# Loading and splitting the first pooled rows inside the scan phase of a hybrid mLSTM and pooling block

## The chip, the cores and the metric

The kernel runs on one core of one Trainium2 chip. The metric is the device time of one execution in microseconds, the median of several runs. All times inside an execution are microseconds from its first instruction.

## What is computed

One layer over 2048 latent tokens of 1024 channels, in float32. A modulated RMSNorm feeds one input projection. Its columns go to two branches: a bidirectional chunked mLSTM scan and a pooling mixer on a grid of 32 x 64 tokens. What matters here is the pooling branch and the merge that follows both:

```python
mixed = (jnp.stack(groups, axis=-2) - pg)                      # four box means of 128 channels each, less the input
mixed = jnp.einsum('btgc,gcd->btgd', mixed, pool_w)            # one 128 x 128 matrix for each group
y_p   = (mixed * pool_scale * silu(z_p)) @ branch_p_w          # 512 -> 1024
hn    = h * rsqrt(mean(h * h) + EPS)                           # by head, h is the scan's output
y_m   = (hn * head_norm_w * sigmoid(o) * silu(z_m)) @ branch_m_w
out   = rmsnorm(x + gate * ((sigmoid(g_m) * y_m + sigmoid(g_p) * y_p) @ out_w))
```

## The kernel before

**Number format.** Every matrix product is made of three passes over fp32r operands: an operand is split into a high part (a copy, mostly by ScalarE) and a low part (the value less its high part, by VectorE or GpSimd), and high by high, high by low and low by high are summed in PSUM. A "split" below is this pair of instructions. Line 42's `f32` only reads such a tile as float32.

**Phases.** The kernel is a row of blocks, and a block ends when all engines have reached its end. The change touches the last two.

**The scan phase** (lines 1545 to 2227) has 136 slots of some 7 us. Slots 8 to 135 each do one step of the mLSTM scan (one head, one direction, one chunk of 128 tokens) and a share of the projection pieces that were left over. In each slot SyncE (SP) issues, in this order, the values and queries of the step three slots on (`values`, `queries`), the scores of that step (`load_scores`), the stores of the pieces that ended in the slot before (`store_piece`), the store of the step before (`store_h`) and the load of the other direction's output for the next step (`other_direction`, L1744). ScalarE prepares the next step's operands, evacuates pieces, writes the high part of the step's weights (`weights_hi`) and then copies the step's result out of PSUM (`ysb`, L1995). VectorE makes the low parts, updates the state and finishes the step (`finish`, whose last instruction L2092 adds the other direction's output). GpSimd computes the four box means one after the other (L2192 to L2227), paced by the steps, and stores each to `mix_d`; the last store is issued in slot 128. After its last slot SP waits until all stores of the projection and of the scan have landed (L1798 to L1801), and only then is its part of the block done.

**The last phase** (lines 2231 to 2926) goes over the tokens in four quarters of 512. A quarter has eight pooled units (the product with `branch_p_w`, one for each 128 channels, 12 matmuls), eight hidden units (with `branch_m_w`, 24 matmuls) and eight output units. Each engine's instructions stand in an order written out by hand. For the first quarter it is this:

- SP loads the pooling weights (`pw`), the pooled rows and their gate rows group by group (`pooled`: `mixt` and `zpt`, two buffers each, L2357 and L2358), and between them the hidden rows (`hidden`, L2344), their gates (`hidden_gate`, `ut`, L2350), the sigmoid gates (`gate_p`, L2370), two tiles of weights (`tile(2)`, `tile(3)`, L2335) and a row of the final norm. The pooled rows of groups 2 and 3 wait until a buffer is free.
- ScalarE writes the high part of `pw`, copies the residual gate's row out of PSUM, then alternates the high parts of the pooled rows (`pooled_hi`, L2614) and of the gated groups (`branch_hi`, L2620). Then come the squares of the first hidden rows (`squares`, L2590 to L2593), their scaling (`normalise`, L2600) and the high part of weight tile 2 (`split_hi`, L2582).
- GpSimd writes the low parts of the pooled rows and of the gated groups (L2899, L2903).
- TensorE turns the residual gate into a row (L2554), multiplies the four groups (`group`, L2467, three matmuls each into two banks in turn), then runs pooled units 0 and 1 (L2475), turns the first hidden rows (`turn_hidden`, L2454), runs units 2 and 3, and so on.
- VectorE writes the low part of `pw`, gates the four groups into one buffer `ypt` (`branch`, L2746; a group waits until the one before is split), and for each pair of units makes the low part of a weight tile (`split_lo`, L2719), applies the sigmoid gates (`gate_pooled`, L2756, which waits for `turn_hidden`) and gates the hidden rows (`gate_hidden`, L2736).

Unit 2 reuses the bank of unit 0, so it waits for `gate_pooled` of unit 0, which stands behind `split_lo` of weight tile 2 on VectorE.

Of the kernel before, what the change touches and what calls it, by code (L numbers as in the profile page):

```python
# [7 lines left out]
FP32 = mybir.dt.float32  # L8
# [3 lines left out]
P = 128  # L12
# [34 lines left out]
def hybrid_block(nc, x, c, ctx, c_ctx, norm_w, ada_w, ada_b, in_w, gate_b, head_norm_w, pool_w,  # L47
# [32 lines left out]
    with ExitStack() as top:  # L80
# [1464 lines left out]
        with ExitStack() as ph:  # L1545
# [8 lines left out]
            QS, KS, VS, SS = 4, 3, 4, 4  # L1554

# [29 lines left out]
            icnt = sb("icnt", [P, 2, GRID_W])  # L1585

# [89 lines left out]
            def _(sp):  # L1676
# [219 lines left out]
            def _(act):  # L1896
# [64 lines left out]
                for t in range(NSLOT):  # L1961
# [266 lines left out]

        late.close()

        with ExitStack() as ph:
# [6 lines left out]
            pw = sb("pw", [P, PG, P])  # L2238
            pw_h = sb("pw_h", [P, PG, P], FP32R)
            pw_l = sb("pw_l", [P, PG, P], FP32R)  # L2240
# [3 lines left out]
            yt = sb("yt", [P, KT, P])  # L2244
            y_h = sb("y_h", [P, KT, TQ], FP32R)
            y_l = sb("y_l", [P, KT, TQ], FP32R)
            mixt = sb("mixt", [P, 2, TQ])
# [8 lines left out]
            m_h = sb("m_h", [P, KT, TQ], FP32R)  # L2256
            m_l = sb("m_l", [P, KT, TQ], FP32R)
            og = sb("og", [P, 2, 2 * P])
# [4 lines left out]
            hss = sb("hss", [P, 4, 2, HEADS])  # L2263
# [5 lines left out]
            rows_loaded = [sem(f"rows_loaded{n}") for n in range(2)]; gate_turned = sem("gate_turned")  # L2269
            gate_ready = sem("gate_ready")   # L2270
            pw_hi = sem("pw_hi"); pw_lo = sem("pw_lo")
# [5 lines left out]
            mix_hi = sem("mix_hi"); mix_lo = sem("mix_lo"); mix_done = sem("mix_done")  # L2277
# [19 lines left out]
            ASIDE = bank[6]  # L2297

# [29 lines left out]
            def _(sp):  # L2328
# [24 lines left out]
                def pooled(i, g):  # L2353
                    n = i * PG + g
                    if n >= 2:
                        sp.wait_ge(yp_made, n - 1)
# [42 lines left out]
                tile(3)  # L2399
                hidden(0, 3)  # L2400
                hidden_gate(0, 1)
                sp.dma_start(fn_row[:, :], final_norm_w.partition_broadcast(P)).then_inc(rows_loaded[1], 16)
# [44 lines left out]
            def _(pe):  # L2447
# [10 lines left out]
                def group(i, g):  # L2458
# [3 lines left out]
                    if c >= 2:  # L2462
                        pe.wait_ge(yp_made, c - 1)
                    if i:
                        pe.wait_ge(p_gated, i * KT)
                    for n, (a, b) in enumerate(((pw_h, mix_h), (pw_h, mix_l), (pw_l, mix_h))):
                        mm = pe.matmul(bank[2 + g % 2][:, :], a[:, g, :], b[:, g % 2, :], start=(n == 0), stop=(n == 2))  # L2467
# [83 lines left out]


# [4 lines left out]
                pe.wait_ge(pw_lo, 1)  # L2557
                for g in range(PG):
                    group(0, g)
# [17 lines left out]
            def _(act):  # L2577
# [31 lines left out]
                def pooled_hi(i, g):  # L2609
                    c = i * PG + g  # L2610
                    act.wait_ge(mix_loaded[g % 2], 32 * (c // 2 + 1))
                    if c >= 2:
                        act.wait_ge(mix_done, c - 1)
                    act.activation(mix_h[:, g % 2], mixt[:, g % 2], ACT.Copy).then_inc(mix_hi, 1)  # L2614

                def branch_hi(i, g):
# [3 lines left out]
                    act.activation(yp_h[:, g], ypt[:, :], ACT.Copy).then_inc(yp_hi, 1)  # L2620
# [26 lines left out]
                act.wait_ge(rows_loaded[0], 16)  # L2647
                act.activation(pw_h[:, :, :], pw[:, :, :], ACT.Copy).then_inc(pw_hi, 1)
                act.wait_ge(gate_turned, 1)
                for b in range(2):  # L2650
                    row = act.activation(gate_row[:, b * TQ:(b + 1) * TQ], bank[6 + b][:, :], ACT.Copy)
                row.then_inc(gate_ready, 1)
                pooled_hi(0, 0)
                pooled_hi(0, 1)
                branch_hi(0, 0)
                pooled_hi(0, 2)
                branch_hi(0, 1)
                pooled_hi(0, 3)
                branch_hi(0, 2)
                squares(0, 0)  # L2660
                branch_hi(0, 3)
                normalise(0, 0)
                for i in range(NTQ):
                    for t in range(NT5):
# [3 lines left out]
                        if t < M0:  # L2668
                            if i == 0:
# [3 lines left out]
                                if t + 1 < QT:  # L2673
                                    normalise(0, t + 1)
                            else:
# [39 lines left out]
            def _(dve):  # L2715
# [24 lines left out]
                def branch(i, g):  # L2740
                    c = i * PG + g
                    dve.wait_ge(mix_done, c + 1)
                    if c:
                        dve.wait_ge(yp_hi, c)
                        dve.wait_ge(yp_lo, c)
                    dve.scalar_tensor_tensor(out=ypt[:, :], in0=bank[2 + g % 2][:, :],  # L2746
                                             scalar=vcol[:, VR["pool"] + g:VR["pool"] + g + 1], in1=zpt[:, g % 2],
                                             op0=ALU.mult, op1=ALU.mult).then_inc(yp_made, 1)
# [81 lines left out]
                dve.wait_ge(pw_hi, 1)  # L2830
                dve.tensor_tensor(pw_l[:, :, :], pw[:, :, :], f32(pw_h[:, :, :]), ALU.subtract).then_inc(pw_lo, 1)
                branch(0, 0)
                branch(0, 1)
                branch(0, 2)
                branch(0, 3)
                norms(0, 0)
                for i in range(NTQ):
                    for t in range(NT5):
# [20 lines left out]
                        elif t < T_O:  # L2859
                            n = t - M0  # L2860
                            if i == 0 and n == 0:
                                dve.wait_ge(rows_loaded[1], 16)
# [28 lines left out]
            def _(pool):  # L2891
# [13 lines left out]
                pooled_lo(0, 0)  # L2905
                pooled_lo(0, 1)
                branch_lo(0, 0)
                pooled_lo(0, 2)
                branch_lo(0, 1)
                pooled_lo(0, 3)  # L2910
                branch_lo(0, 2)
                branch_lo(0, 3)
# [39 lines left out]
```

## Time and profile before

| | us |
|---|---|
| median of 3 runs | 2403.62 (2403.3 to 2408.27) |
| profiled execution, its own time | 2401.29 |
| its span, first to last instruction | 2399.5 |
| TensorE busy in the span | 2274.2 (95%) |
| VectorE, ScalarE, GpSimd busy | 1494.0, 972.8, 610.1 |
| data moved by DMA | 501.66 MB, 209 GB/s on average |

The profiled execution is one run, and its span is 1.79 us shorter than its own time. The page cuts the span into 40 slices of 60 us. TensorE is busy for nine tenths or more in most of them; two of the few exceptions after the start, with busy shares of six and nine tenths and a clock of seven tenths in the first, hold the end of the scan phase and the start of the last phase, around 1860 us.

### The profile page before, as it was taken

The numbers are of one execution on the slowest core, as the hardware profiler recorded it, in microseconds if no ns is written. First come the engines' busy times: TensorE is split into PE (matmuls) and PEld (weight loads), VectorE is DVE, ScalarE is ACT, GpSimd is POOL, SyncE is SP. The second block draws the span as 40 slices with busy tenths as digits, with TensorE's granted clock in tenths as the row PEclk, the third lists the DMA queues.
The fourth block names the chain that finished last, engine by engine and source line by source line (L and its number), as shares of the span: only waits on it lengthen the run. The fifth ranks groups of instructions, "written<-read, shape, count | busy, mean of one in ns | idle before, by whom it ended". The sixth has DMA issues, their size and how long they took to land. (4 is left out here: it accounts for less than half of the span.)

```text
span 2399.5 us, 35270 instructions
## 1 busy us (share of the span) xinstructions
PE 2274.2 (95%) x12251; PEld 1934.1 (81%) x12251; DVE 1494.0 (62%) x2660; ACT 972.8 (41%) x1982; POOL 610.1 (25%) x545
## 2 busy tenths in 40 slices
PE   7799999989999989999999999999999699999998
PEld 5588888767887878888888888888887488888878
DVE  5545567875766646575767566767675355646564
ACT  6323355542332323434444344444443535252532
POOL 0223344533445421121122112321220212020210
PEclk9899999999999999999999999999999799999999
DMA  9466698876788666666776877666665665757562
GB/s 273 143 154 176 180 250 242 255 218 136 192 201 249 163 223 224 222 221 215 233 250 201 274 262 250 224 221 200 227 211 188 206 192 158 234 171 226 187 207 100
DMA packets 399266, 501.66 MB, mean 209 GB/s; under 512 B 25800, under 2 KB 283380, under 8 KB 393588
## 3 DMA queue, kind: packets, MB, share of 16 engines
q1 hardware_dynamic: 334836, 377.76, 48.0%
q10 hardware_dynamic: 55136, 83.90, 14.0%
q0 software_dynamic: 9120, 37.75, 6.0%
q8 instruction: 101, 1.65, 0.3%
q14 instruction: 73, 0.60, 0.1%
HBM read 352.82 MB, written 163.27 MB: 215 GB/s over the span
## 5 line engine op out<-in xcount | busy, mean ns | idle before, releaser
L1867 PE MATMUL bank<-xlate,wh 128*128 128x512 f32 x2048 | 670.4, 401 | 10.1 <-DVE v_t L2001 6.3
L1867 PEld LDWEIGHTS bank<-xlate,wh 128*128 128x128 f32 x2048 | 373.1, 189 | 79.4 <-DVE v_t L2001 6.7
L1867 PE MATMUL bank<-xlate,wl 128*128 128x512 f32 x1024 | 409.6, 400 | 0.0
L1016 PE MATMUL bank<-xlate,wh 128*128 128x512 f32 x1024 | 330.4, 396 | 5.8 <-DVE wl L1288 4.9
L1016 PE MATMUL bank<-xtop,wh 128*128 128x512 f32 x768 | 250.6, 403 | 9.9 <-DVE wl L1288 9.9
L1016 PEld LDWEIGHTS bank<-xlate,wh 128*128 128x128 f32 x1024 | 191.1, 189 | 48.1 <-ACT wh L1068 4.7
L1867 PEld LDWEIGHTS bank<-xlate,wl 128*128 128x128 f32 x1024 | 193.4, 189 | 34.1
L1016 PE MATMUL bank<-xlate,wl 128*128 128x512 f32 x512 | 201.4, 393 | 0.0
L1016 PEld LDWEIGHTS bank<-xtop,wh 128*128 128x128 f32 x768 | 144.2, 192 | 41.8 <-ACT wh L1068 10.8
L2024 DVE SCALAR_TENSOR_TENSOR state<-state,cols,bank 128x516 f32<-128x516 f32 x128 | 95.7, 748 | 112.0 <-PE bank L1828 111.9
L1016 PE MATMUL bank<-xtop,wl 128*128 128x512 f32 x384 | 152.7, 398 | 0.0
L1312 DVE SCALAR_TENSOR_TENSOR tmp<-bank,psum 128x512 f32<-128x512 f32 x112 | 76.9, 687 | 104.3 <-PE bank L1016 64.0
L1995 ACT ACTIVATE ysb<-bank 128x258 f32<-128x258 f32 x128 | 49.5, 387 | 197.4 <-PE bank L1828 196.9
L2029 DVE TENSOR_TENSOR wl<-wraw,wh 128x1024 fp32r<-128x1024 f32 x62 | 77.2, 1245 | 67.6 <-ACT wh L1915 67.6
L917 POOL TENSOR_TENSOR os<-tmp,os 128x512 fp32r<-128x512 f32 x64 | 90.1, 1412 | 111.6 <-ACT os L1177 111.5
L1068 ACT ACTIVATE wh<-ssum 128x512 fp32r<-128x512 f32 x96 | 60.4, 629 | 138.9 <-PE bank L1016 75.2
L1841 PE MATMUL bank<-state_h,q_t 128*128 128x258 f32 x512 | 113.0, 283 | 2.6 <-DVE den L2081 2.6
L1016 PEld LDWEIGHTS bank<-xlate,wl 128*128 128x128 f32 x512 | 96.6, 189 | 21.7
L1828 PE MATMUL bank<-v_t,ek_h 128*128 128x258 f32 x576 | 110.3, 283 | 1.7 <-DVE ek_l L2006 1.7
L1288 DVE TENSOR_TENSOR wl<-ssum,wh 128x512 fp32r<-128x512 f32 x96 | 78.7, 820 | 44.9 <-ACT wh L1068 44.7
L1932 ACT ACTIVATE s_t<-bank 128x128 f32<-128x128 f32 x64 | 17.7, 277 | 193.6 <-PE bank L1818 193.5
L1841 PEld LDWEIGHTS bank<-state_h,q_t 128*128 128x128 f32 x512 | 87.5, 189 | 8.9 <-issue 3.3
(321 smaller groups left out, 5351.4 us busy)
## 6 DMA issues: line engine op xcount, KB each, us to landing
v_t<-vk_d SPq DMA_DIRECT2D x144, 384.0 KB, 3.8
qk_d<-os SPq DMA_DIRECT2D x32, 1024.0 KB, 5.7
q_t<-qk_d SPq DMA_DIRECT2D x128, 256.0 KB, 4.1
wraw<-wpair_d ACTq DMA_DIRECT2D x31, 1024.0 KB, 6.6
rawb<-in_in_w_dram ACTq DMA_DIRECT2D x64, 256.0 KB, 5.4
vk_d<-os SPq DMA_DIRECT2D x16, 1024.0 KB, 4.6
wpair_d<-in_in_w_dram POOLq DMA_DIRECT2D x64, 256.0 KB, 6.1
k_t<-qk_d SPq DMA_DIRECT2D x64, 256.0 KB, 5.0
```

What stands on the lines that cost most here:

```text
L917: pool.tensor_tensor(part[:, :, 1, :], tmp[:, a % NTM].rearrange("p (c t) -> p c t", t=P), f32(part[:, :, 0, :]), ALU.subtract).then_inc(q ...
L1016: mm = pe.matmul(dst[:, :], a[:, kd, :], x_block(part, XB[name])[:, kd], start=(kd == 0 and n == 0), stop=(kd == KH - 1 and n == 2))
L1068: act.activation(op_ring(wh, p), op_source(u, name), ACT.Copy).then_inc(op_hi, 1)
L1288: dve.tensor_tensor(op_ring(wl, p), op_source(u, name), f32(op_ring(wh, p)), ALU.subtract).then_inc(op_lo, 1)
L1312: return dve.scalar_tensor_tensor(out=dst, in0=src[:, :], scalar=kscale(u), in1=in1, op0=ALU.mult, op1=ALU.add)
L1828: mm = pe.matmul(ubank[:, b, 0:VW], e_[:, L, b * P:(b + 1) * P], v_t[:, V, va, :], start=(n == 0), stop=(n == 2))
L1841: pe.matmul(XBANK[:, 0:VW], q_t[:, l % QS, b, qa, :], c_[:, L, b, :], start=(b == 0 and n == 0), stop=(b == HB - 1 and n == 2))
L1867: mm = pe.matmul(bank[m % 2][:, :], a[:, u % 2, k, :], xlate[part][:, BLOCK_OF[k // KH, tq], k % KH], start=(k == 0 and n == 0), stop=(k = ...
L1932: act.activation(s_t[:, l % SS, :], SBANK[l % 2][:, 0:P], ACT.Copy).then_inc(s_copied, 1)
L1995: act.activation(ysb[:, :], YBANK[:, 0:VW], ACT.Copy).then_inc(y_read, 1)
L2024: dve.scalar_tensor_tensor(out=state[:, ch], in0=state[:, ch], scalar=col(d, NC + latent_chunk(l), 4, h), in1=upair[:, :, 0:VW], op0=ALU.m ...
L2029: dve.tensor_tensor(wl[:, u % 2], wpair[:, :, u % 2 * P:(u % 2 + 1) * P], f32(wh[:, u % 2]), ALU.subtract).then_inc(w_lo, 1)
```

## The change

Loads, splits and order of the first quarter's pooled part change; all quarters after it stay as they were.

- In slots 128, 129 and 130 SP also issues the loads of `pw` (256 KB), of the first quarter's pooled rows of all four groups (`mixq`, 1 MB) and of their gate rows (`zpq`, 1 MB), into scan buffers that are no longer used. The second waits for the last store of GpSimd to `mix_d`, the third for the last use of the buffer that it overwrites.
- ScalarE writes the high part of `pw` in slot 130 and of the four groups in slots 131 to 134, between `weights_hi` and the copy to `ysb`. GpSimd, whose box means are done, writes the five low parts.
- At the scan's end SP waits only for one of the two sets of step stores. The last step's store is waited for in the last phase, behind the load of the first `hidden_gate` and ahead of the first `hidden`.
- In the last phase TensorE does the four groups first, into four banks (2, 3, 0, 1), without waits between them, and then the residual gate's rows. VectorE gates a group in place (`zpq`) and writes its low part itself (`first_branch_lo`); ScalarE writes only the high parts of the gated groups, and copies the residual gate's row after the fourth hidden rows. GpSimd has nothing to do until the hidden rows.
- SP's order becomes: `hidden_gate(0,0)`, the wait, `hidden(0,0)`, `hidden(0,1)`, `gate_p(0,0)`, `gate_p(0,1)`, `hidden_gate(0,1)`, `tile(2)`, `hidden(0,2)`, `tile(3)`, `hidden(0,3)`, the final norm's row.

```diff
+            HEAD_AT, HEAD_SPLIT = NSLOT - 8, NSLOT - 5
@@ sync, scan phase
+                    if t == HEAD_AT:
+                        sp.wait_ge(s_done, NHALF)
+                        sp.dma_start(pw[:, :, :], pool_w[0].rearrange("g c n -> c g n")).then_inc(pw_loaded, 16)
+                    if t == HEAD_AT + 1:
+                        sp.wait_ge(mix_stored, 16 * PG)
+                        sp.dma_start(mixq[:, :, :], mix_d[:, :, 0:TQ].rearrange("g p t -> p g t")).then_inc(mixq_loaded, 16)
+                    if t == HEAD_AT + 2:
+                        sp.wait_ge(u_made, nz[-1])
+                        sp.dma_start(zpq[:, :, :], zp_d[:, :, 0:TQ].rearrange("g p t -> p g t")).then_inc(zpq_loaded, 16)
...
-                    sp.wait_ge(h_stored[n], 16 * NL // 2)
+                sp.wait_ge(h_stored[NL % 2], 16 * NL // 2)
@@ scalar, scan phase, after weights_hi
+                    if t == HEAD_SPLIT - 1:
+                        act.wait_ge(pw_loaded, 16)
+                        act.activation(pw_h[:, :, :], pw[:, :, :], ACT.Copy).then_inc(pw_hi, 1)
+                    if 0 <= t - HEAD_SPLIT < PG:
+                        g = t - HEAD_SPLIT
+                        act.wait_ge(mixq_loaded, 16)
+                        act.activation(mixq_h[:, g], mixq[:, g], ACT.Copy).then_inc(mix_hi, 1)
@@ gpsimd, scan phase, at the end
+                pool.wait_ge(pw_hi, 1)
+                pool.tensor_tensor(pw_l[:, :, :], pw[:, :, :], f32(pw_h[:, :, :]), ALU.subtract).then_inc(pw_lo, 1)
+                for g in range(PG):
+                    pool.wait_ge(mix_hi, g + 1)
+                    pool.tensor_tensor(mixq_l[:, g], mixq[:, g], f32(mixq_h[:, g]), ALU.subtract).then_inc(mix_lo, 1)
@@ sync, last phase
-                sp.dma_start(pw[:, :, :], pool_w[0].rearrange("g c n -> c g n")).then_inc(rows_loaded[0], 16)
-                pooled(0, 0)
-                pooled(0, 1)
+                hidden_gate(0, 0)
+                sp.wait_ge(h_stored[(NL - 1) % 2], 16 * NL // 2)
                 hidden(0, 0)
                 hidden(0, 1)
-                hidden_gate(0, 0)
                 gate_p(0, 0)
                 gate_p(0, 1)
-                pooled(0, 2)
+                hidden_gate(0, 1)
+                tile(2)
                 hidden(0, 2)
-                pooled(0, 3)
-                tile(2)
                 tile(3)
                 hidden(0, 3)
-                hidden_gate(0, 1)
@@ tensor, last phase
+            def group_bank(i, g):
+                return bank[2 + g % 2] if i else bank[(2, 3, 0, 1)[g]]
...
+                pe.wait_ge(pw_lo, 1)
+                for g in range(PG):
+                    group(0, g)
                 for j in range(KT):
                     mm = pe.matmul(bank[6 + j // 4][:, j % 4 * P:(j % 4 + 1) * P], mgate[:, j:j + 1].broadcast_to([P, P]),
                                    ident[:, :], start=True, stop=True)
                 mm.then_inc(gate_turned, 1)
-                pe.wait_ge(pw_lo, 1)
-                for g in range(PG):
-                    group(0, g)
@@ scalar, last phase
-                pooled_hi(0, 0) ... branch_hi(0, 3), with squares(0, 0) ahead of the last
+                for g in range(PG):
+                    branch_hi(0, g)
                 squares(0, 0)
+                act.wait_ge(yp_lo, PG)
                 normalise(0, 0)
@@ vector, last phase
+                def first_branch_lo(g):
+                    dve.wait_ge(yp_hi, g + 1)
+                    dve.wait_ge(yp_made, g + 1)
+                    dve.tensor_tensor(yp_l[:, g], zpq[:, g], f32(yp_h[:, g]), ALU.subtract).then_inc(yp_lo, 1)
...
                 branch(0, 0)
                 branch(0, 1)
-                branch(0, 2)
-                branch(0, 3)
+                for g in range(PG):
+                    first_branch_lo(g)
+                    if g + 2 < PG:
+                        branch(0, g + 2)
                 norms(0, 0)
```

## Rows read from the trace of the kernel before

**Rows 1.** Windows: us, busy us (count) of each engine, clock, DMA share, GB/s.
```profile
1859.70:1883.60 23.90, 8.61 (x25) 5.98 (x25) 2.94 (x4) 6.73 (x14) 7.58 (x7) 0.57 0.93 288
1859.70:1893.90 34.20, 17.89 (x60) 13.12 (x60) 5.96 (x10) 14.31 (x34) 10.05 (x8) 0.64 0.76 237
```

**Rows 2.** Chain of waits that ended last, around 1860: start us, us, what.
```profile
1860.72 5.45 DMA zpt<-zp_d
...
1873.99 7.58 DMA zpt<-zp_d
```

**Rows 3.** Timeline of SP's queue: start us, us, engine line op.
```profile
1857.57 0.32 SPq L1738 DMA_DIRECT2D hsum_d<-num  x1
1859.73 0.39 SPq L2387 DMA_DIRECT2D pw<-in_pool_w_dram  x1
```

**Rows 4.** DMA issues, 1855 to 1887 and 1798 to 1830: KB each, us to landing.
```profile
hsum_d<-num SPq DMA_DIRECT2D x1, 128.0 KB, 1.7
...
mix_d<-pool_a POOLq DMA_DIRECT2D x1, 1024.0 KB, 9.9
```

**Rows 5.** Timeline of TensorE, start of the last phase.
```profile
1859.77 3.75 PE L2554 MATMUL bank<-ident,mgate 128*128 128x128 f32 x16 [5.47 <-PEq L1545]
1868.31 0.77 PE L2467 MATMUL bank<-mix_h,pw_h 128*128 128x512 f32 x1 [4.79 <-POOL mix_l L2899]
...
1891.94 1.03 PE L2454 MATMUL bank<-ident,hsum 128*128 128x128 f32 x8
1893.95 0.47 PE L2475 MATMUL bank<-yp_h,wh 128*128 128x512 f32 x1 [0.98 <-DVE hsum L2756]
```

**Rows 6.** Timeline of ScalarE, start of the last phase.
```profile
1870.75 0.63 ACT L2620 ACTIVATE yp_h<-ypt 128x512 fp32r<-128x512 f32 x1 [1.69 <-DVE ypt L2746]
...
1882.64 0.40 ACT L2590 ACTIVATE junk_h<-hsum 128x256 bf16<-128x256 f32 x1
...
1886.81 1.69 ACT L2600 ACTIVATE hsum<-hsum,hss 128x256 f32<-128x256 f32 x4
1888.41 1.04 ACT L2582 ACTIVATE wh_c<-wraw 128x1024 fp32r<-128x1024 f32 x1
```

**Rows 7.** Timeline of VectorE, start of the last phase.
```profile
1869.96 0.75 DVE L2746 SCALAR_TENSOR_TENSOR ypt<-bank,vcol,zpt 128x512 f32<-128x512 f32 x1 [6.29 <-PE bank L2467]
...
1889.48 1.23 DVE L2719 TENSOR_TENSOR wl_c<-wraw,wh_c 128x1024 fp32r<-128x1024 f32 x1 [2.89 <-ACT wh_c L2582]
1893.11 1.28 DVE L2756 SCALAR_TENSOR_TENSOR hsum<-gt,bank 128x512 f32<-128x512 f32 x2 [2.40 <-PE bank L2454]
1900.65 1.28 DVE L2756 SCALAR_TENSOR_TENSOR hsum<-gt,bank 128x512 f32<-128x512 f32 x2
```

**Rows 8.** Windows of the scan's last slots, columns as in rows 1.
```profile
1800.00:1815.00 15.00, 15.00 (x81) 12.89 (x80) 8.29 (x23) 4.81 (x12) 0.43 (x1) 1.00 0.96 326
1815.00:1830.00 15.00, 15.00 (x81) 12.91 (x80) 10.30 (x24) 6.68 (x14) 0.00 (x0) 1.00 0.57 190
```

**Rows 9.** Timelines of GpSimd, SP, VectorE and ScalarE in the scan's last slots.
```profile
1799.83 0.59 POOL L2226 DMA_DIRECT2D mix_d<-pool_a  x1 [0.30 <-POOL pool_a L2224]
...
1814.91 0.43 SPq L1744 DMA_DIRECT2D hother<-h_d  x1
...
1827.99 0.49 DVE L2092 SCALAR_TENSOR_TENSOR num<-num,den,hother 128x256 f32<-128x256 f32 x1
...
1826.17 0.39 ACT L1995 ACTIVATE ysb<-bank 128x258 f32<-128x258 f32 x1 [1.23 <-PE bank L1828]
```

**Rows 10.** Windows where TensorE's granted clock changes, columns as in rows 1.
```profile
1854.30:1856.70 2.40, 0.00 (x0) 0.00 (x0) 2.33 (x5) 0.39 (x1) 0.00 (x0) 1.00 0.15 57
1856.70:1863.40 6.70, 3.63 (x16) 3.48 (x16) 1.19 (x4) 0.63 (x1) 0.00 (x0) 0.50 0.39 113
```

**Rows 11.** Timelines of GpSimd and VectorE: two splits at the same time.
```profile
1919.44 2.34 POOL L2894 TENSOR_TENSOR y_l<-yt,y_h 128x1024 fp32r<-128x1024 f32 x1 [4.97 <-ACT y_h L2607]
...
1920.34 2.52 DVE L2719 TENSOR_TENSOR wl_c<-wraw,wh_c 128x1024 fp32r<-128x1024 f32 x1 [2.07 <-ACT wh_c L2582]
```

More of the change, by code:

```diff
@@ L1585, in hybrid_block @@
             icnt = sb("icnt", [P, 2, GRID_W])
+            zpq = nc.alloc_sbuf_tensor_at("zpq", [P, PG, TQ], FP32, offset=TANH_AT)
+            pw = nc.alloc_sbuf_tensor_at("pw", [P, PG, P], FP32, offset=KEYS_AT)
+            pw_h = nc.alloc_sbuf_tensor_at("pw_h", [P, PG, P], FP32R, offset=KEYS_AT + PG * P * 4)
+            pw_l = nc.alloc_sbuf_tensor_at("pw_l", [P, PG, P], FP32R, offset=KEYS_AT + 2 * PG * P * 4)
+            mixq = nc.alloc_sbuf_tensor_at("mixq", [P, PG, TQ], FP32, offset=POOL_AT)
+            mixq_h = nc.alloc_sbuf_tensor_at("mixq_h", [P, PG, TQ], FP32R, offset=POOL_AT + PG * TQ * 4)
+            mixq_l = nc.alloc_sbuf_tensor_at("mixq_l", [P, PG, TQ], FP32R, offset=POOL_AT + 2 * PG * TQ * 4)
+            pw_loaded = sem("pw_loaded"); zpq_loaded = sem("zpq_loaded"); mixq_loaded = sem("mixq_loaded")
+            pw_hi = sem("pw_hi"); pw_lo = sem("pw_lo"); mix_hi = sem("mix_hi"); mix_lo = sem("mix_lo")
             piece_done = sem("piece4_done")
@@ L2244, in hybrid_block @@
             yt = sb("yt", [P, KT, P])
+            og = sb("og", [P, 2, 2 * P])
+            hss = sb("hss", [P, 4, 2, HEADS])
+            pad5 = sb("pad5", [P, 16])
+            pw_place = sb("pw_place", [P, 3, PG, P])
             y_h = sb("y_h", [P, KT, TQ], FP32R)
             y_l = sb("y_l", [P, KT, TQ], FP32R)
+            m_h = sb("m_h", [P, KT, TQ], FP32R)
+            m_l = sb("m_l", [P, KT, TQ], FP32R)
             mixt = sb("mixt", [P, 2, TQ])
@@ L2268, in hybrid_block @@
             unit_done = sem("unit_done")
-            rows_loaded = [sem(f"rows_loaded{n}") for n in range(2)]; gate_turned = sem("gate_turned")
+            rows_loaded = sem("rows_loaded"); gate_turned = sem("gate_turned")
             gate_ready = sem("gate_ready")
-            pw_hi = sem("pw_hi"); pw_lo = sem("pw_lo")
             h_loaded = [sem(f"h_loaded{n}") for n in range(QT)]
@@ L2354, in pooled @@
                     n = i * PG + g
[L2355 removed]
+                    if n >= PG + 2:
                         sp.wait_ge(yp_made, n - 1)
@@ L2461, in group @@
                     pe.wait_ge(mix_lo, c + 1)
-                    if c >= 2:
+                    if i:
                         pe.wait_ge(yp_made, c - 1)
-                    if i:
                         pe.wait_ge(p_gated, i * KT)
-                    for n, (a, b) in enumerate(((pw_h, mix_h), (pw_h, mix_l), (pw_l, mix_h))):
-                        mm = pe.matmul(bank[2 + g % 2][:, :], a[:, g, :], b[:, g % 2, :], start=(n == 0), stop=(n == 2))
+                    h, l, at = (mix_h, mix_l, g % 2) if i else (mixq_h, mixq_l, g)
+                    for n, (a, b) in enumerate(((pw_h, h), (pw_h, l), (pw_l, h))):
+                        mm = pe.matmul(group_bank(i, g)[:, :], a[:, g, :], b[:, at, :], start=(n == 0), stop=(n == 2))
                     mm.then_inc(mix_done, 1)
@@ L2645, in tail_root @@
                     act.activation(oss[:, 2, q:q + 1], oss[:, 1, q:q + 1], ACT.Sqrt).then_inc(tail_act, 1)
[L2647 to L2659, printed above, removed]
+                for g in range(PG):
+                    branch_hi(0, g)
                 squares(0, 0)
-                branch_hi(0, 3)
+                act.wait_ge(yp_lo, PG)
                 normalise(0, 0)
@@ L2674, in _ @@
                                     normalise(0, t + 1)
+                                if t == M0 - 1:
+                                    act.wait_ge(gate_turned, 1)
+                                    for b in range(2):
+                                        row = act.activation(gate_row[:, b * TQ:(b + 1) * TQ], bank[6 + b][:, :], ACT.Copy)
+                                    row.then_inc(gate_ready, 1)
                             else:
@@ L2742, in branch @@
                     dve.wait_ge(mix_done, c + 1)
-                    if c:
+                    scale = vcol[:, VR["pool"] + g:VR["pool"] + g + 1]
+                    if i:
                         dve.wait_ge(yp_hi, c)
                         dve.wait_ge(yp_lo, c)
-                    dve.scalar_tensor_tensor(out=ypt[:, :], in0=bank[2 + g % 2][:, :],
-                                             scalar=vcol[:, VR["pool"] + g:VR["pool"] + g + 1], in1=zpt[:, g % 2],
-                                             op0=ALU.mult, op1=ALU.mult).then_inc(yp_made, 1)
+                        dve.scalar_tensor_tensor(out=ypt[:, :], in0=group_bank(i, g)[:, :], scalar=scale, in1=zpt[:, g % 2],
+                                                 op0=ALU.mult, op1=ALU.mult).then_inc(yp_made, 1)
+                    else:
+                        if g == 0:
+                            dve.wait_ge(zpq_loaded, 16)
+                        dve.scalar_tensor_tensor(out=zpq[:, g], in0=group_bank(i, g)[:, :], scalar=scale, in1=zpq[:, g],
+                                                 op0=ALU.mult, op1=ALU.mult).then_inc(yp_made, 1)
+                def first_branch_lo(g):
+                    dve.wait_ge(yp_hi, g + 1)
+                    dve.wait_ge(yp_made, g + 1)
+                    dve.tensor_tensor(yp_l[:, g], zpq[:, g], f32(yp_h[:, g]), ALU.subtract).then_inc(yp_lo, 1)
                 def gate_pooled(i, n):
```

30 lines of the change are left out of this document (7 added, 23 removed).

## The prediction

> **What bounds the kernel now.** TensorE is busy for 95% of the span, so a gain can only come from a stretch in which it waits. I read the page's 40 slices first: the weak one is where the scan ends. Then the windows of that stretch: from the last phase's first instruction at 1859.70 to 1883.60 the DMA engines are 0.93 busy while TensorE has 8.61 us of work in 23.90, at a mean clock of 0.57 [rows 1]. Then the chain of waits: between 1860 and 1886 its longest members are two landings of `zpt`, 5.45 and 7.58 us, the gate rows of groups 0 and 3 [rows 2]; the splits of the four groups hang between them. So the stretch is bound by loads and by small steps that depend on them. From pooled unit 2 on (1893.95 [rows 5]) each pair of units is paced by TensorE and by a ring through ScalarE and VectorE that the change leaves alone. The working therefore asks one question: when does pooled unit 2 start after the change?
>
> **Step 1, the scan's end.** Before, the last step's store goes out at 1857.57 [rows 3] and lands 1.7 us later [rows 4], at 1859.27; SP's first issue of the new phase follows at 1859.73 [rows 3], 0.46 later. After, SP waits for the landing of older stores only: its queue is free at 1857.57 + 0.32 = 1857.89, and the phase starts at 1858.35, 1.38 us earlier. The bounds of this step are 0, if another engine holds the block, and 1.38; I take 1.38, since VectorE's last scan instruction is what SP's last store waits for. TensorE starts 0.04 behind SP, as before: 1858.39.
>
> **Step 2, the groups.** Nothing that they need is still to come, and each has a bank of its own. TensorE's clock has fallen by then: after 2.4 us of idling it went to 1.2 GHz, and came back 3.6 us after work began again (1859.77 to 1863.4 [rows 5, 10]). 512 columns at 1.2 GHz are 0.427 us, a group of three 1.28. From a group's start to VectorE's gating is 1.65 us (1868.31 to 1869.96 [rows 5, 7]): group 0 is gated at 1860.04, group 3, three times 1.28 later, at 1863.88. The low parts that VectorE now makes lie between: four gatings of 0.75 and four low parts of about half of 1.23 [rows 7] are 5.5 us, and the last ends near 1866. From gating to high part is 0.79 us (1869.96 to 1870.75 [rows 6, 7]), so ScalarE's last high part, 0.63 long [rows 6], runs from 1864.67 to 1865.3. TensorE meanwhile: the 12 group matmuls to about 1862.9 (the clock is back at 1862.0), the 16 of the residual gate (3.75 us at the low clock [rows 5], so 1.9) to 1864.8, and 24 matmuls of units 0 and 1 at 512 columns / 2.4 GHz, 5.1 us, to 1869.9, with no wait inside, as the fourth split is read some 2 us into unit 0.
>
> **Step 3, from the squares to unit 2.** Before, ScalarE began the squares at 1882.64, the scaling at 1886.81 (4.17 later) and weight tile 2 at 1888.41 (1.60 later) [rows 6]; VectorE's low part began 1.07 later, at 1889.48, for 1.23 [rows 7]. After, `gate_pooled` comes directly behind it, and unit 2 starts 0.84 after that (1893.11 to 1893.95 [rows 5, 7]). Sum: 4.17 + 1.60 + 1.07 + 1.23 + 0.84 = 8.91. From 1865.3 that is 1874.2. TensorE's turn (1.03 us [rows 5]) can only begin when the scaling ends, 1871.1; it ends at 1872.1, and TensorE idles 2.1 us, less than the 2.4 after which the clock fell. The copies of the residual gate's row, moved behind the fourth hidden rows, cost nothing: ScalarE waits there, and their first reader is the first merge. Without that cover it would be twice 0.63 at most.
>
> **Step 4, the loads.** The first 3.15 MB in SP's new order (`ut`, two `hsum`, two `gt`, `ut`, weight tile 2) must land before 1871.1. A store of 0.13 MB took 1.7 us [rows 4], of which 0.45 are bytes at 288 GB/s, so I let 1.2 us pass before the first bytes: 1859.55. At 288 GB/s, the rate of the saturated stretch [rows 1], 3.15 MB take 10.9 us: 1870.5, early by 0.6. At 237, the mean of the longer stretch [rows 1], 13.3: 1872.85, late by 1.8. I take the first, since the queue stays full; more speed gains nothing, as ScalarE comes later. The first `hsum` (1.05 MB with `ut`) is there at 1863.2, ahead of the squares. The sigmoid gate of unit 2, 6.03 MB in all with the final norm's row and weight tile 4, lands at 1880.5, against a use 6.70 us after unit 2's start (1893.95 to 1900.65 [rows 5, 7]), 1880.9. These two margins, 0.6 and 0.4, are the thin part of the forecast.
>
> **Step 5, what the scan pays.** ScalarE gets five high parts of 0.63, GpSimd five low parts of about half of 2.34 [rows 11], SP three issues. ScalarE idles 1.23 us ahead of `ysb` in a slot that also splits a weight tile [rows 9], which hides one high part; without that, 5 x 0.63 = 3.2. SP's wait in slot 129: the store to `mix_d` goes out at 1799.83 [rows 9] and lands 9.9 us later [rows 4], near 1810. Queued behind the wait are the issues of slot 130; the last of them, the other direction's rows, went out at 1814.91 and is used by the instruction at 1827.99 [rows 9], 13.1 us later. The 2.36 MB of loads are 8.2 us at 288 GB/s. The DMA engines are 0.96 busy from 1800 to 1815 and 0.57 from there to 1830 [rows 8]: 0.6 us are free in the first stretch, 6.4 in the second, so transfers of these slots may land some 4 us later; with the 7.58 of a queued load [rows 2] that is 11.6, within 13.1. Bounds: 0 and 8.2. I take 0, as TensorE is busy without a gap through the saturated 15 us [rows 8].
>
> **The sum.** Unit 2 starts at 1874.2 in place of 1893.95: 19.7 us, 1.4 from step 1 and 18.3 from steps 2 to 4. The profiled execution's own time, 2401.29, would be 2381.6. The median of the runs is 2403.62, 2.3 above that execution, so I predict 2383.9.
>
> **A rule against it.** VectorE's split of a weight tile took 2.52 us while GpSimd's split of hidden rows ran beside it [rows 11], and 1.23 alone [rows 7]. The Trainium skill, in "GPSIMD Engine Reference", section "1. Specifications", has the reason: GpSimd shares its SBUF interfaces with VectorE, and they contend when a VectorE instruction has two SBUF inputs. By that rule, the trace agrees. Five GpSimd splits in the scan could then hold VectorE; what that gives is rival 3.
>
> **The rivals.** (1) *The loads set the start.* At 237 GB/s unit 2's gate lands at 1859.55 + 25.4 = 1885.0, 4.1 late; TensorE idles over 2.4 us, its clock falls, and half of 3.6 us, 1.8, is lost. Gain 13.8: 2389.8. For it: SP's list leaves no slack, and the final norm's row lies ahead of that gate. Against it: 2.36 MB that were loaded here are gone. (2) *The waits only move.* If `mixq` lands after slot 131's high part is due, near 1825, ScalarE stands ahead of `ysb` and the scan is late one for one; the gain is gone if it lands at 1845. With 9.9 for the store and 7.58 for a queued load [rows 2, 4] it lands at 1817. Time: 2403.6. (3) *GpSimd holds VectorE in the scan.* Five times 1.29 (2.52 less 1.23), all on the path: gain 13.3, 2390.3. Against it: VectorE has 8.29 us of work in 15 [rows 8], and GpSimd starts when ScalarE's high part ends, in the slot's idle time. (4) *Slower: the early loads starve the scan.* If in each of slots 129 to 135 the other direction's rows land later than their lead of 13.1 us by 2.4 or more, TensorE idles, its clock falls and 1.8 is lost at half speed: 7 x 4.2 = 29.4 lost against 19.7 won, 2413.3. It decides from a landing of 15.5 us. Against it: 7.58 was the longest landing of the chain in a full queue [rows 2]. The Trainium skill, in "DMA: Bandwidth & Descriptors", section "Queues, rings and completion order", speaks for it: a completion is counted only after all earlier writes of the same DMA engine, so a small load waits for the whole megabyte ahead of it. No run here shows that by itself.
>
> **How the numbers follow.** Forecast, a gain of 16 to 23: 0.76, by itself 2380 to 2388. Rival 1: 0.12. Rival 2: 0.03. Rival 3: 0.04. Rival 4: 0.03. The last 0.02 is a small gain of any other cause. Within 0.2% (4.8 us, about what a measurement of this kernel can tell from no change) are rival 2 and half of the last: 0.04. Slower is rival 4: 0.03. Faster is the rest: 0.93. The range: at best TensorE alone sets the pace, and unit 2 starts at 1869.9 + 1.03 + 0.98 [rows 5] = 1871.9, a gain of 22 and 2379.3 from the profiled execution; at the other end stand rivals 1 and 3, 2390.3. So 2379 to 2391.
>
> **What would show it.** Right: SP's first issue of the last phase 0.8 us after the last step's store goes out; 12 group matmuls in a row; no landing of pooled rows in the chain before the second quarter; unit 2 some 16 us after the phase's first instruction, where it was 34 before; the scan's slots as long as before. Wrong, step by step: a longer gap at the block's end (step 1), waits of TensorE between the groups (2), weight tile 2 or the gates landing after ScalarE and VectorE ask for them (4), TensorE idling in slots 129 to 135 (5).

## The result and the profile after

Six runs of each kernel: 2390.87 us after (2386.77 to 2395.74) against 2405.69 before, a ratio of 0.9942, 95% interval 0.9929 to 0.9956. The forecast was 2383.9, with 2379 to 2391. The direction and the place were right, the size was not: 14.8 us instead of 19.7, and below the 16 to 23 to which the prediction gave 0.76. The profiled execution of the changed kernel took 2392.69 us, span 2390.9.

In this execution the scan ran 2.72 us later than in the profile of before, already ahead of its first changed load (the store to `mix_d` went out at 1802.56, where it was 1799.83 [rows 9]), so 2.72 is taken off when times of the two are compared. The head of the last phase first. SP's queue, which answers to [rows 3]:

```profile
1860.29 0.32 SPq L1754 DMA_DIRECT2D hsum_d<-num  x1
1861.20 0.37 SPq L2394 DMA_DIRECT2D ut<-u_d  x1
```

From the last store to the first issue 0.91 us, where it was 2.16. TensorE's timeline, which answers to [rows 5]:

```profile
1861.39 0.77 PE L2509 MATMUL bank<-mixq_h,pw_h 128*128 128x512 f32 x1 [4.37 <-PEq L1545]
1861.95 0.63 PE L2509 MATMUL bank<-mixq_l,pw_h 128*128 128x512 f32 x1
...
1866.22 0.63 PE L2509 MATMUL bank<-mixq_h,pw_l 128*128 128x512 f32 x1
1866.64 2.00 PE L2599 MATMUL bank<-ident,mgate 128*128 128x128 f32 x16
...
1877.03 0.47 PE L2517 MATMUL bank<-yp_h,wh 128*128 128x512 f32 x1 [1.91 <-DVE hsum L2804]
```

The groups follow one another without a wait, and unit 2 starts at 1877.03, or 1874.31 on the clock of before: 19.6 us earlier than 1893.95 [rows 5]. ScalarE, which answers to [rows 6], and VectorE, to [rows 7]:

```profile
1867.67 0.63 ACT L2662 ACTIVATE yp_h<-zpq 128x512 fp32r<-128x512 f32 x1 [0.65 <-DVE zpq L2790]
1868.21 0.40 ACT L2632 ACTIVATE junk_h<-hsum 128x256 bf16<-128x256 f32 x1
...
1872.15 1.71 ACT L2642 ACTIVATE hsum<-hsum,hss 128x256 f32<-128x256 f32 x4 [0.30 <-DVE hss L2763]
1873.97 1.06 ACT L2624 ACTIVATE wh_c<-wraw 128x1024 fp32r<-128x1024 f32 x1
```

```profile
1875.06 1.23 DVE L2756 TENSOR_TENSOR wl_c<-wraw,wh_c 128x1024 fp32r<-128x1024 f32 x1 [3.01 <-ACT wh_c L2624]
1876.20 1.28 DVE L2804 SCALAR_TENSOR_TENSOR hsum<-gt,bank 128x512 f32<-128x512 f32 x2
```

The loss lies behind this. The window of the second quarter's hidden units, first before, then after (us, busy us and count of PE, PEld, DVE, ACT, POOL, clock, DMA share, GB/s):

```profile
2048.88:2092.42 43.54, 43.54 (x194) 36.03 (x192) 30.12 (x36) 11.08 (x14) 0.00 (x0) 1.00 0.72 236
```

```profile
2035.35:2080.15 44.80, 44.80 (x193) 36.10 (x192) 30.11 (x36) 11.08 (x14) 0.00 (x0) 1.00 0.72 234
```

TensorE's groups in the same two windows, before and after (busy us, mean ns of one, idle us):

```profile
L2475 PE MATMUL bank<-y_h,wh 128*128 128x512 f32 x32 | 12.5, 389 | 0.0
...
L2475 PE MATMUL bank<-y_h,wh_c 128*128 128x512 f32 x32 | 12.4, 389 | 0.0
```

```profile
L2517 PE MATMUL bank<-y_h,wh 128*128 128x512 f32 x32 | 12.7, 396 | 0.0
...
L2517 PE MATMUL bank<-y_h,wh_c 128*128 128x512 f32 x32 | 12.7, 396 | 0.0
```

The reader is to see that nothing differs but TensorE's own speed: no idle time, clock 1.00 (2.4 GHz), the same 192 products, the same work of the other engines, the same transfer rate, and still 1.26 us more. That is 44.80 / 192 = 233.3 ns from one matmul's start to the next instead of 226.8. The last block of output units goes the other way (before, then after):

```profile
2342.62:2388.85 46.23, 46.23 (x385) 46.02 (x383) 21.77 (x32) 11.73 (x21) 0.00 (x0) 1.00 0.24 75
```

```profile
2334.79:2380.18 45.39, 45.39 (x385) 45.18 (x383) 21.59 (x32) 11.62 (x21) 0.00 (x0) 1.00 0.24 76
```

The second place is the clock. Windows around the first hidden unit, before and after (columns as above), and one stretch of output units after:

```profile
1915.65:1918.90 3.25, 0.00 (x1) 0.00 (x0) 2.62 (x5) 0.59 (x1) 0.00 (x0) 0.88 0.54 152
1918.90:1921.90 3.00, 0.00 (x0) 0.01 (x1) 1.56 (x1) 1.41 (x2) 2.34 (x1) 0.50 0.03 10
1921.90:1924.90 3.00, 2.98 (x7) 2.42 (x8) 0.96 (x1) 0.00 (x0) 0.00 (x0) 0.50 0.20 62
```

```profile
1904.60:1905.40 0.80, 0.00 (x0) 0.01 (x1) 0.63 (x1) 0.14 (x1) 0.67 (x1) 0.50 0.00 0
1905.40:1911.10 5.70, 5.68 (x13) 4.50 (x14) 0.96 (x1) 0.00 (x0) 0.00 (x0) 0.50 0.57 182
...
2255.80:2259.30 3.50, 3.50 (x19) 3.50 (x18) 2.15 (x1) 1.31 (x2) 2.41 (x1) 0.51 0.03 7
```

In both kernels TensorE stands 6.3 us ahead of the first hidden unit, and the clock falls to 1.2 GHz in that wait. Before, more than half of the low stretch lay in the wait itself; after, it began later and 5.7 us of it fell on work.

From the first hidden unit to TensorE's end it is 466.93 us before and 474.76 after, +7.83. At full clock: hidden units 4 x 1.26 = 5.04, pooled units of three quarters +0.42, last output block -0.84, together 4.62. At low clock: 2.40 - 1.26 = 1.14 at the first hidden unit, and +1.84 for the third output block, which holds the low stretch shown last. The other two output blocks: +0.23. The gain at the first hidden unit was still 19.2 (1921.92 against 1905.42 - 2.72).

### The profile page after: what moved, and what is told of

Read it like the earlier page. It is cut to its first block, busy times and chain, and to the rows that moved or that the text cites. A ratio compares the mean times of both kernels' runs of the same rounds, so it can differ in the third digit from the quotient of the medians.

```text
span 2390.9 us, 35262 instructions
## 1 busy us (share of the span) xinstructions
PE 2273.2 (95%) x12251; PEld 1928.8 (81%) x12251; DVE 1502.7 (63%) x2663; ACT 971.6 (41%) x1982; POOL 609.5 (25%) x542
## 4 chain that ended last, share of the span: by engine, by line
PE 51%; ACT 4%; DVE 3%; DMA 3%; issue 2%; SPq 1%; POOL 0%; DVEq 0%; ACTq 0%
PE bank L1896 29%; PE bank L2517 9%; PE bank L1857 4%; PE bank L1870 4%; PE bank L2572 2%; PE bank L1878 2%; PE bank L1847 1%; ACT junk_h L2632 1%; DVE wl L2756 1%; ACT hsum L2642 1%; ACT wh_c L2624 1%; ACT wh L2624 1%; DVE yt L2773 0%; DMA zpt<-zp_d 0%; ACT junk_o L2678 0%
## 5 line engine op out<-in xcount | busy, mean ns | idle before, releaser
L2090 DVE TENSOR_TENSOR p_l<-wexp,p_h 128x128 fp32r<-128x128 f32 x128 | 72.9, 570 | 36.8 <-ACT p_h L1965 36.8
```

The source lines that it names most:

```text
L2090: dve.tensor_tensor(p_l[:, l % 2, :], wexp[:, l % 2, :], f32(p_h[:, l % 2, :]), ALU.subtract).then_inc(p_lo, 1)
```

## Experiments

The section on the change says that all later quarters stay as they were, and its cut of the diff leaves out one place. The tiles of the last phase lie in another order, with three of them now ahead of `y_h`:

```
             yt = sb("yt", [P, KT, P])
+            og = sb("og", [P, 2, 2 * P])
+            hss = sb("hss", [P, 4, 2, HEADS])
+            pad5 = sb("pad5", [P, 16])
```

These are 2048 + 128 + 64 = 2240 bytes in each partition. `y`, `yp` and `m` below are the rows that hidden, pooled and output units read, each a high and a low part (`y_h`, `y_l`) with the same start modulo 256; "at 160" means a start 160 bytes behind a multiple of 256, unless another modulus is named. Before, `y`, `yp`, `m` and the weights of these units all start at 160; after, the first three start at 96.

The main theory: the tiles that the change moved in SBUF (`y_h` by 2240 bytes, and the tiles behind it) make TensorE read slower, whatever the order of work. Rivals: the new order of loads and splits disturbs TensorE; or the clock alone, which differs from run to run. "Spacing" below is the mean time from one matmul's start to the next, the slowest tenth (low clock, waits) left out.

**a_again.** No edit.

> The changed kernel once more, unedited, beside the kernel before on the same chip. In its first profile the 288 matmuls of 512 columns in a quarter's pooled and hidden units began 233.3 ns apart (226.7 in the kernel before) and those of the output units 117.8 (119.8). If that spacing belongs to the kernel, it is 233 and 118 here again, and the ratio is about 0.994. If it was a passing state of that one run, it is 227 and 120 here and the time falls to about 2386.

2392.36 us, ratio 0.9936 (0.9916 to 0.9956); spacing 233.0 and 117.3. The spacing belongs to the kernel and not to one run.

**a_pad1856 and a_pad64.** Unused bytes, nothing else moves in time:

```
             pw_place = sb("pw_place", [P, 3, PG, P])
+            pad6 = sb("pad6", [P, 464])      # a_pad64: [P, 16]
             y_h = sb("y_h", [P, KT, TQ], FP32R)
-            ypt = sb("ypt", [P, TQ])         # a_pad1856 alone: room
+            ypt = nc.alloc_sbuf_tensor_at("ypt", [P, TQ], FP32, offset=KEYS_AT)
```

> The changed kernel with 1856 unused bytes ahead of y_h, so that y_h, y_l, yp_h, yp_l, m_h and m_l start at the same SBUF address modulo 2048 as in the kernel before (ypt moves into the dead raw pool weights to make room); no instruction is added, removed or reordered. Address theory: the pooled and hidden units go back to 227 ns a matmul and the output units to 120; 4 quarters x (288 x 6.6 - 384 x 2.0 ns) = 4.5 us faster than the changed kernel, about 2386. Traffic theory (the new order of loads and splits slows TensorE's operand reads): 233 and 118 stay, time unchanged near 2391.

> The changed kernel with 64 unused bytes ahead of y_h: the start is then as in the kernel before modulo 128 and 256 bytes, but not modulo 512 or more. Address theory with a period of 256 bytes or less: 227 and 120 ns as in the kernel before, about 2386. Address theory with a longer period: another spacing, 233 and 118 or a third pair. Traffic theory: 233 and 118, about 2391.

Both went back to 226.6 and 119.7 ns, and hidden units to 43.54 us. The traffic theory falls: the order of loads and splits is the changed kernel's, and the spacing is that of before. In time 2387.27 (0.9925, 0.9901 to 0.9948) and 2390.7 (0.9939, 0.9914 to 0.9963): 5.1 and 1.7 below a_again, with intervals that overlap. The second quarter of a_pad64:

```profile
2038.68:2082.22 43.54, 43.54 (x193) 36.04 (x192) 30.15 (x36) 11.08 (x14) 0.00 (x0) 1.00 0.73 235
```

**b_pad192.** The same addresses given to the kernel before, alone:

```
             yt = sb("yt", [P, KT, P])
+            pad6 = sb("pad6", [P, 48])
             y_h = sb("y_h", [P, KT, TQ], FP32R)
```

> The kernel before, nothing changed but 192 unused bytes ahead of y_h, which puts y_h, y_l, yp_h, yp_l, m_h and m_l at the changed kernel's address modulo 2048. Address theory: its pooled and hidden units go from 227 to 233 ns a matmul, its output units from 120 to 118, and it is 4.5 us slower than the kernel before, a ratio of 1.002. Traffic theory: 227 and 120 stay and the ratio is 1.000.

Spacing 233.0 and 117.1, ratio 1.0022 (1.0006 to 1.0039): 192 unused bytes cost 5.3 us, 1.4 to 9.4. Its second quarter is as long as the changed kernel's:

```profile
2051.69:2096.49 44.80, 44.80 (x194) 35.90 (x192) 30.17 (x36) 11.07 (x14) 0.00 (x0) 1.00 0.72 234
```

**c_0_64, c_64_0, c_16_80.** Which places are slow? The same edit with pads ahead of `y_h` and `yp_h`, in c_16_80 ahead of `m_h` too; one run each.

> The changed kernel with unused bytes that put y_h, y_l and m_h, m_l at 0 and yp_h, yp_l at 64 bytes modulo 128 (32 in the kernel before, 96 in the changed one; the weights stay at 32). If the spacing depends on where the moving operand starts within 64 bytes (32 in both kernels so far, which differ by 64), 0 and 64 behave alike; if within 128 bytes, y (0) and yp (64) differ from each other. No value of ours for either: 227 or 233 ns if only the upper half of the 128 bytes is slow, below 227 if 32 is itself a costly place. The output units, m at 0: 120 ns if like m at 32, 118 if like m at 96.

> The same with y_h, y_l, m_h, m_l at 64 and yp_h, yp_l at 0 bytes modulo 128: if the address alone sets the spacing, the values of y and yp in the run before change places; if the operand's shape or the unit's length did, they stay where they are.

> The same with y_h, y_l at 16, m_h, m_l at 112 and yp_h, yp_l at 80 bytes modulo 128. If the halves of 128 bytes decide, y is near 227 and yp near 233 ns, and the output units near 118. A start that is no multiple of 32 bytes may cost something of its own: a third value, above 233.

y and yp at 0 or 64 modulo 128: 233.0 to 233.3 ns in both runs, at either place. c_16_80 did not test what its name says. A tile's start is rounded up to a multiple of 32 bytes when the program is built, so behind the pad of 48 bytes `y_h` starts at byte 99488, which is 32 modulo 128, and m at 0 and yp at 96 modulo 256 follow from it; its last output block takes 45.22 us, as e_place's does with m at 0. y has 226.6 there and yp 233.1, as at these places in other runs; a start off 32 bytes was not measured. Modulo 128, 32 was quick so far and 0, 64 and 96 slow.

**d_fullwait.** Step 1 undone in the changed kernel:

```
-                sp.wait_ge(h_stored[NL % 2], 16 * NL // 2)
+                for n in range(2):
+                    sp.wait_ge(h_stored[n], 16 * NL // 2)
```

> The changed kernel with the wait for the stores of both directions of h put back at the scan's end (step 1 undone, everything else kept). By step 1 the first group matmul then comes 1.4 us later after the last scan matmul: 5.7 to 5.8 us behind its end instead of 4.4. If the last store's receipt is waited for anyway by what follows, 4.4 stays.

```profile
1863.27 0.77 PE L2510 MATMUL bank<-mixq_h,pw_h 128*128 128x512 f32 x1 [5.64 <-PEq L1545]
```

One run: the idle time ahead of the first group is 5.64 us instead of 4.37: 1.27, forecast 1.38.

**a_again2, a_pad64b, e_place.** The price of the spacing once more, and a placement that by a period of 128 bytes should be quick everywhere (y and yp at 32, m at 0 modulo 128).

> The changed kernel unedited, as the base that the next three are held against on this chip: 233 and 118 ns, a ratio of 0.994 to the kernel before.

> The changed kernel with 64 unused bytes ahead of y_h once more, with more rounds, to price the spacing in time: 227 and 120 ns, so 4 x (40.2 + 26.8 us of pooled and hidden units shortened by 6.6 of 233.3 ns, less what the output units lose) = 3.5 to 4.5 us below the changed kernel by the address theory, a ratio of 0.992 to 0.9925. If the loss behind unit 2 came from TensorE's clock alone, the spacing goes back and the time does not: 0.994.

> The changed kernel with unused bytes that put y_h, y_l, yp_h, yp_l at 32 and m_h, m_l at 0 bytes modulo 128, so that each kind of unit has the shorter spacing seen so far: 227 ns in the pooled and hidden units and 116.4 in the output units. By the address theory 384 x 3.5 ns x 4 = 5.4 us less than with 64 bytes, at most (the output units also wait for other engines), and 9 us less than the changed kernel: a ratio of 0.990. If the waits in the output units take the gain, 0.992.

2392.94 (0.9944, 0.9923 to 0.9966), 2390.0 (0.9932, 0.9911 to 0.9953), 2388.29 (0.9924, 0.9902 to 0.9947). The 64 bytes are worth 2.9 us here by the medians, with intervals that overlap again, and less than the 3.5 to 4.5 expected. a_pad64b's profile shows two low stretches in its output blocks, a_again2's one; that the waits between output units take some back too is not shown. e_place's expectation missed, in time (a ratio of 0.990 or 0.992) and in spacing: yp at 32 modulo 128 had 231.9 ns. It is 32 modulo 256 there, where y is 160. So the period is not 128, and a_pad64, whose `y_h` lies 2304 bytes behind that of the kernel before, points to 256.

**f_place_turn.** e_place, and the last hidden rows gated ahead of the pooled gates:

```
+                                if t == M0 - 1:
+                                    gate_hidden(0, t)
+                                    gate_pooled(0, 2 * t)
+                                    dve.wait_ge(y_hi, QT)
+                                    dve.tensor_tensor(y_l[:, :, t * P:QT * P], yt[:, :, :], f32(y_h[:, :, t * P:QT * P]),
+                                                      ALU.subtract).then_inc(y_lo, 1)
+                                    gate_pooled(0, 2 * t + 1)
...
-                for q in range(QT):
+                for q in range(QT - 1):
                     hidden_lo(0, q)
```

> The run before this one, and the last quarter-row of the first quarter is gated ahead of the two pooled gates, with its low part y_l made by VectorE in place of GpSimd. TensorE's idle time ahead of the first hidden unit, 6.3 us in every kernel so far, should fall by 1.3 (gates behind) + 1.2 (2.4 us on GpSimd against 1.2 on VectorE) = 2.5 us, so a ratio of 0.989; if the clock does not fall in the shorter wait, the 13 matmuls after it that ran at 1.2 GHz gain up to 2.5 us more.

TensorE's first hidden unit, in the changed kernel and then here:

```profile
1905.42 0.77 PE L2517 MATMUL bank<-y_h,wh 128*128 128x512 f32 x1 [6.31 <-POOL y_l L2942]
...
1905.32 0.47 PE L2520 MATMUL bank<-y_h,wh 128*128 128x512 f32 x1 [3.82 <-DVE y_l L2899]
```

The wait fell from 6.31 to 3.82 us, the 2.5 expected, and the low clock on work behind it from 5.7 to 3.4. Time 2386.83, 0.9918 (0.9894 to 0.9943): by the medians 1.5 below e_place, and not the ratio of 0.989 that was expected.

**g_whc64.** Own address, or distance from the weights? One run, with y and yp at 160 and m at 128. The unused 64 bytes `pad5` go ahead of `wh_c`, so that only one of the two weight pairs moves (`wh_c` and `wl_c`, to 224):

```
+            pad5 = sb("pad5", [P, 16])
             wh_c = sb("wh_c", [P, 2, KT, P], FP32R)
...
-            pad5 = sb("pad5", [P, 16])
```

> The changed kernel with y_h, y_l, yp_h, yp_l at 160 and m_h, m_l at 128 modulo 256, and the copy pair wh_c, wl_c alone moved up by 64 bytes (224 modulo 256), while wh, wl stay at 160. If the moving operand's own address sets the spacing, all 512-column units have 227 ns, those on wh and those on wh_c. If it is its distance from the weights, units on wh have 227 ns and units on wh_c 233. Either way yp at 160 is at 227 where 32 gave 232, so the period is 256 bytes and not 128; if yp stays at 232, the period is longer.

The window of its second quarter's hidden units, and TensorE's groups in it:

```profile
2033.70:2077.90 44.20, 44.20 (x194) 36.06 (x192) 30.15 (x36) 11.08 (x14) 0.00 (x0) 1.00 0.73 237
```

```profile
L2520 PE MATMUL bank<-y_h,wh_c 128*128 128x512 f32 x32 | 12.7, 396 | 0.0
L2520 PE MATMUL bank<-y_l,wh_c 128*128 128x512 f32 x32 | 12.7, 396 | 0.0
...
L2520 PE MATMUL bank<-y_h,wl 128*128 128x512 f32 x32 | 12.5, 389 | 0.0
L2520 PE MATMUL bank<-y_h,wh 128*128 128x512 f32 x32 | 12.5, 389 | 0.0
```

The same `y_h`, in one execution, is 389 ns against `wh` (same place modulo 256) and 396 against `wh_c` (64 bytes on). So the moving operand's own address does not decide it; the pair does. 44.20 is near the middle of 43.54 and 44.80. The output units show the same: with m at 128 the spacing is 116.6 to 116.8 ns against `wh` and `wl` and 119.1 to 120.1 against `wh_c` and `wl_c`, and the last output block takes 45.71 us, where it is 44.97 with all weights at 160 (g_place_turn). That the distance within the pair decides, and not a place of its own for each of the two, fits all runs but is not shown: no run moved both operands of such units by the same bytes.

**g_place_turn.** f_place_turn with yp at 160 and m at 128 modulo 256 (the pad ahead of `m_h` is `[P, 56]` instead of `[P, 24]`).

> The version with the last quarter-row gated first and its y_l on VectorE, now with yp_h, yp_l at 160 and m_h, m_l at 128 modulo 256: 227 ns for pooled and hidden units, 116.4 for output units. By the places' spacing 4 x 384 x 1.3 ns = 2 us below the same version with m at 0, of which the waits between the output units may take half: a ratio of 0.991 to 0.9915, about 2385.

Spacing 226.6, 227.6 (yp) and 116.4. Time 2384.05, 0.9903 (0.9888 to 0.9917): better than both kernels, by its interval against before below that of the changed one. Its last output block:

```profile
2325.59:2370.56 44.97, 44.97 (x385) 44.76 (x383) 21.54 (x32) 11.72 (x21) 0.00 (x0) 1.00 0.25 76
```

**b_again, b_again2.** The kernel before, unedited.

> The kernel before once more, for its clock. Its first profile shows no stretch at 1.2 GHz in the three blocks of output units that hold the turns, and seven of the nine profiles of kernels with the new head show 3.4 us of it in one of them or more. If that stretch comes with the change, it is absent here again; if the first profile was one without it by chance, one of these two repeats has it, 1.7 us each.

> The kernel before a third time, with the same expectation as the run ahead of it.

In the output blocks b_again has no low stretch, b_again2 10.2 us in all (of the profiles of the new head, 13 of 14 in the end have at least one, so the count in that expectation was low):

```profile
2000.90:2007.80 6.90, 6.07 (x26) 5.81 (x27) 4.36 (x8) 3.64 (x12) 0.73 (x1) 0.51 0.73 241
2151.20:2154.60 3.40, 3.40 (x18) 3.40 (x17) 2.25 (x1) 1.11 (x2) 2.38 (x1) 0.51 0.02 5
```

So the stretches occur without the change. The four profiles with the old head have it in two. Whether the change makes it more frequent stays open. The repeats show something else: from the last scan matmul to the first hidden unit they took 66.35 and 66.13 us, the profile that the forecast stands on 67.62. That run was late in its head and free of low stretches behind it.

## Why the forecast was right up to unit 2 and wrong behind it

**Step 1** held: 4.37 us idle ahead of the first group, and undone 1.27 more (forecast 1.38).

**Step 2** held where it counts. The forecast had set the gatings of the four groups one slow group, 1.28 us, apart, and so the first and the last came:

```profile
1863.05 0.75 DVE L2790 SCALAR_TENSOR_TENSOR zpq<-bank,vcol,zpq 128x512 f32<-128x512 f32 x1 [2.78 <-PE bank L2509]
...
1866.88 0.75 DVE L2790 SCALAR_TENSOR_TENSOR zpq<-bank,vcol,zpq 128x512 f32<-128x512 f32 x1
```

The squares began at 1868.21 - 2.72 = 1865.5 (forecast 1865.3). The low parts took 0.68, near the half of 1.23. TensorE's groups ended 1.2 us later than worked out, since the clock was low up to 1866.8, 5.4 us from their start and not 3.6; units 0 and 1 still ended ahead of what unit 2 waits for. The 2.4 us of idling after which the clock fell before, which step 3 and rival 1 use as a limit, are one execution's: here it fell 2.9 us into the wait, and in c_64_0 it stayed at 1.00 through 4.37 us of waiting and 0.7 us of work, and read 0.50 from 1864.9 on.

**Step 3** held: from the squares to unit 2 8.82 us (1868.21 to 1877.03), forecast 8.91; TensorE idle 1.91 ahead of it, forecast 2.1.

**Step 4** held with no margin. Weight tile 2 is in the chain, and lands just before ScalarE takes it (start us, us, what):

```profile
1864.32 9.63 DMA wraw<-in_branch_p_w_dram
1873.95 0.02 issue
1873.97 1.07 ACT wh_c L2624
```

That is 1871.2 on the clock of before, 0.7 later than forecast. ScalarE finished the scaling at 1873.86, 0.1 earlier, so the load decides by 0.1. The second thin margin held too: unit 2's sigmoid gates landed at 1882.72, and VectorE used them at 1883.87. That unit 2 agrees to 0.1 us is in part luck: this load came 0.7 late where 0.6 were free.

**Step 5** held: TensorE has no gap in slots 129 to 135. GpSimd's splits did slow VectorE beside them, as rival 3 had it: a subtraction that takes 0.29 us alone took 1.38 in three slots, one of them here,

```profile
1821.33 1.38 DVE L2090 TENSOR_TENSOR p_l<-wexp,p_h 128x128 fp32r<-128x128 f32 x1
```

but VectorE had that time to spare, and the price did not come. The early loads took 8.2 (`mixq`) and 9.8 us (`zpq`), and the other direction's rows of slots 129 to 135 landed 6.5 us after their issue at the latest, far from the 15.5 of rival 4.

**The step that failed** is a sentence ahead of the steps: from unit 2 on the work is paced "by TensorE and by a ring through ScalarE and VectorE that the change leaves alone". The sum made unit 2's gain the whole kernel's. Order and counts of that work were left alone; the places of its operands were not, and so TensorE's own pace was not. The term that the sum put at nothing is 5.04 + 0.42 - 0.84 = 4.6 us at full clock; put in alone into the kernel before, it measured 5.3 (1.4 to 9.4), and taken out of the changed kernel 1.7 to 5.1 by the medians of three pairs of runs, whose intervals overlap. With it the forecast would have been a gain of 15.1, where 14.8 was measured (10.6 to 17.1 by the interval), and a time near 2388.5. Of the 2.4 us that remain in time, 2.1 are the median of the kernel before, 2405.69 in six runs where the forecast stood on 2403.62 in three.

Two more things are seen in the profiles and are too small for that interval. The forecast's one execution had a head 1.3 to 1.5 us longer than two repeats, so that some 18 and not 19.2 were there to be won. And the low clock at the first hidden unit cost 1.1 more than in that execution, but only 0.5 more than in the repeats, whose first hidden block took 45.71 and 45.66 us (before 45.05, after 47.46). The range, too, stood on two bases: its lower end on the profiled execution, its upper end on the median.

None of the rivals describes what happened: rival 1 and rival 3 gave a time near the measured one (2389.8 and 2390.3), for other reasons.

## What to carry to other kernels

A change that adds, drops or reorders tiles moves every tile behind them, and on stages that TensorE fills without a gap that can be a price of its own: compare the length of an untouched block before comparing anything else. Where hundreds of matmuls use the same pair of operands, try other starts of the two modulo 256 bytes, and read the built addresses, not the pads. A pad adds no instruction, and 64 bytes were worth 1.7 and 2.9 us here by the medians. And take the gain of a head from more than one profile of before.

## What the runs showed of the hardware

Spacing at 2.4 GHz by the start of the operands modulo 256, with the weights at 160. Moving operand of 512 columns: at 160 226.6 ns (yp 227.3 to 227.7); at 32 231.9; at 0, 96, 128 and 192 233.0 to 233.3. In the output units, where m is stationary and the weights move with 256 columns, the same place is the slow one: m at 160 119.7 to 119.9, at 0, 96 and 192 117.1 to 117.9, at 128 116.4 to 116.6. With the weights at 224 (g_whc64) y and yp at 160 had 233.0 to 233.3, and m at 128 had 119.1 to 120.1. A start that is equal to the old one modulo 256 (a_pad64) gave the same spacing as one equal modulo 2048 (a_pad1856). Why the sign turns is open; starts off 32 bytes and other strides were not tried.

The Trainium skill, in "TensorE: Matmul & The Clock Gate", section "Step-by-step: what each phase is for", says that TensorE has two independent SBUF read ports, one for the streaming operand and one for the weights. That gives no reason why the places of the two should matter together; g_whc64 measured 389 against 396 ns for the same moving tile, so here the measurement decides.
